# A hybrid encoder trunk on one core: the sample's down products as seven block products per pair of f tiles, and another order of the sample's last norm

## What is computed

```python
D_MODEL = 1024
D_FF = 2816
...
    h = _rmsnorm(x, norm_ffn_g)
    u = jnp.einsum('bsd,df->bsf', h, w_up)
    up = jnp.pad(u, ((0, 0), (1, 1), (0, 0)))
    u = up[:, :-2] * conv_w[0] + up[:, 1:-1] * conv_w[1] + up[:, 2:] * conv_w[2] + conv_b
    a, b = jnp.split(u, 2, axis=-1)
    x = x + jnp.einsum('bsf,fd->bsd', jax.nn.silu(a) * b, w_down)
    return x
...
    return _rmsnorm(x, final_norm_g)
```

## Time and profile before

| | us |
|---|---|
| three runs, median (lowest to highest) | 2393.9 (2391.09 to 2394.6) |
| the profiled execution, its own time | 2391.54 |
| span of the profiled execution | 2389.6 |
| mean granted TensorE clock in it | 0.997 of full speed |

### The profile page before, as it was taken

The page is one execution under the profiler, slowest core; times in us unless marked ns, Lnnn a source line. Parts: engine busy times, 40 slices in busy tenths (PEclk is TensorE's granted clock), DMA queues, the critical chain, the costliest instruction groups (busy, mean ns, idle before and its releaser), DMA issues.

```text
span 2389.6 us, 34203 instructions
## 1 busy us (share of the span) xinstructions
PE 2329.2 (97%) x12186; PEld 1993.3 (83%) x12186; DVE 1798.9 (75%) x2627; ACT 1092.8 (46%) x2147; POOL 1288.7 (54%) x1497
## 2 busy tenths in 40 slices
PE   7999999999999989999999999999989999999998
PEld 6998898888998968888878888888868888888886
DVE  7537777788889967566653379987768888888888
ACT  4426665656678852122332233433244444444444
POOL 5444635588877712043151055555556666666663
PEclk9999999999999999999999999999999999999999
DMA  8744434432222049888873342232253333332332
GB/s 296 250 172 149 159 131 159 154 143 104 79 79 85 13 151 313 305 285 296 281 259 132 106 150 97 89 106 97 84 202 94 97 93 102 93 102 93 100 95 110
DMA packets 153415, 352.69 MB, mean 148 GB/s; under 512 B 15776, under 2 KB 50976, under 8 KB 142752
## 3 DMA queue, kind: packets, MB, share of 16 engines
q1 hardware_dynamic: 151952, 350.12, 43.0%
q10 hardware_dynamic: 1296, 0.39, 0.1%
HBM read 268.67 MB, written 81.79 MB: 147 GB/s over the span
## 4 chain that ended last, share of the span: by engine, by line
PE 57%; DVE 3%; DMA 1%; POOL 1%; issue 1%; SPq 1%; ACT 0%; DVEq 0%; POOLq 0%; ACTq 0%
PE r_bank L2183 29%; PE r_bank L2060 10%; PE r_bank L2089 9%; PE r_bank L2122 5%; PE r_bank L2141 1%; PE r_bank L2170 1%; PE r_bank L2104 1%; DMA r_wxq_raw<-in_w_xq_heads 0%; DVE r_conv L2617 0%; DVE r_block L2610 0%; DVE r_prob L2598 0%; PE r_bank L2153 0%; DVE r_x_p L2833 0%; DVE r_x_p L2850 0%; POOL r_wxq_lo L1900 0%
## 5 line engine op out<-in xcount | busy, mean ns | idle before, releaser
L843 PE MATMUL t_proj<-t_w_hi,t_hbuf 128*128 128x384 f32 x1056 | 311.7, 348 | 2.1 <-ACT t_nat L994 0.7
L2705 DVE TENSOR_TENSOR r_x_p<-r_bank,r_x_p 128x512 f32<-128x512 f32 x280 | 183.0, 683 | 47.9 <-PE r_bank L2183 46.8
L1153 DVE TENSOR_REDUCE t_max_neg<-t_scores 128x1 f32<-128x1024 f32 (+1 forms) x192 | 197.0, 1038 | 23.8 <-PE t_scores L877 17.9
L1017 ACT ACTIVATE t_prob<-t_scores,t_max_neg 128x1024 f32<-128x1024 f32 (+1 forms) x192 | 187.4, 978 | 49.7 <-DVE t_max_neg L1153 45.5
L843 PEld LDWEIGHTS t_proj<-t_w_hi,t_hbuf 128*128 128x128 f32 x1056 | 194.9, 189 | 8.3 <-issue 6.8
L1026 ACT CAST t_pt_hi<-t_turn 128x512 fp32r<-128x512 f32 x240 | 140.3, 587 | 107.5 <-PE t_turn L896 82.3
L1173 DVE TENSOR_TENSOR t_pt_lo<-t_turn,t_pt_hi 128x512 fp32r<-128x512 f32 x240 | 163.5, 686 | 29.9 <-ACT t_pt_hi L1026 26.1
L843 PE MATMUL t_proj<-t_w_lo,t_hbuf 128*128 128x384 f32 x528 | 177.9, 337 | 0.0
L2617 DVE SCALAR_TENSOR_TENSOR r_conv<-r_rows,r_taps,r_conv 128x511 f32<-128x511 f32 (+3 forms) x134 | 157.0, 1172 | 27.0 <-ACT r_conv L2415 24.6
L1933 POOL TENSOR_TENSOR r_w_lo<-r_stage,r_w_hi 128x1024 fp32r<-128x1024 f32 x42 | 100.9, 2403 | 129.3 <-ACT r_w_hi L2354 129.3
L1949 POOL TENSOR_TENSOR r_s_lo<-r_s_raw,r_s_hi 128x512 fp32r<-128x512 f32 x87 | 131.7, 1519 | 63.2 <-ACT r_s_hi L2359 63.2
(11 more groups left out here) (318 smaller groups left out, 7315.2 us busy)
## 6 DMA issues: line engine op xcount, KB each, us to landing
t_hbuf<-split_x SPq DMA_DIRECT2D x60, 1024.0 KB, 4.8
block_sums<-r_block SPq DMA_DIRECT2D x128, 256.0 KB, 3.7
r_block<-in_w_up_units SPq DMA_DIRECT2D x88, 256.0 KB, 5.1
r_stage<-in_w_up_units SPq DMA_DIRECT2D x44, 512.0 KB, 3.3
r_s_raw<-block_sums SPq DMA_DIRECT2D x87, 256.0 KB, 2.7
r_w_raw<-in_w_up_units SPq DMA_DIRECT2D x66, 256.0 KB, 2.6
split_x<-t_hbuf SPq DMA_DIRECT2D x12, 1024.0 KB, 5.3
r_stage<-in_w_down SPq DMA_DIRECT2D x22, 512.0 KB, 3.3
```

Of the source, the lines that this page charges most:

```text
L843: ins = nc.tensor.matmul(proj_bank(i), l, r[:, k, :], start=(k == 0 and j == 0), stop=(k == KT - 1 and j == 2))
L1017: nc.scalar.activation(prob[:, n % PSLOTS, 0:p.keys], ps_s[:, n % 2, 0:p.keys], ACT.Exp, bias=max_neg[:, n % COLS:n % COLS + 1], accum_out ...
L1153: nc.vector.tensor_reduce(max_neg[:, n % COLS:n % COLS + 1], ps_s[:, n % 2, 0:p.keys], AX.X, ALU.max, negate=True).then_inc(max_done, 1)
L2705: nc.vector.tensor_tensor(x_p[:, t, cols], down_bank(q), x_p[:, t, cols], ALU.add).then_inc(p_add, 1)
```

## The change

- Sample's down products of f tiles 0 to 19 are made per pair of f tiles, as seven block products (`sample_pair`): f tiles 2m and 2m+1 by token halves (two tiles of 128 tokens) by column halves, 6 matmuls of 512 columns each. p7, p1, p4 and p6 are woven into the second up product of f tile 2m+2 after blocks 1, 3, 5 and 7, and p5, p2 and p3 into that of f tile 2m+3 after blocks 1, 3 and 5. For the last pair these three stand in the first up product of f tile 21. f tiles 20 and 21 keep the eight plain products.
- Their weights are the block sums that prompt uses too, and plain blocks, 512 wide, through three slots (`sd_raw/hi/lo`): load (`load_s`), cast on ScalarE (`s_high`), low part on GpSimd (`s_low`). A load waits until the product three weights before it is through. `split_down` is gone.
- Their left sides are halves of the gated products, now kept for two f tiles in `s_g`, and four sums of them by GpSimd (`b_sums`, 256 wide), with seven casts (`b_high`, ScalarE) and seven low parts (`b_low`, VectorE), 256 wide, per pair. `sg_hi` and `sg_lo` stay for f tiles 20 and 21 alone.
- VectorE's adds: 14 per pair in place of 16. In f tile 1, which has no down products now, the four operand steps follow each other.
- Last norm: tiles 2 and 3 are squared, scaled and sent first, then 0 and 1, whose scalings stand behind `subtract_w22(1)` and behind the value shifts of f tile 1. Prompt's first down load no longer waits for sent tiles; the next two wait for tile 0 and tile 1. The low part of prompt's first sum (`a_low(0, "s3")`) moves to behind the last scaling.

VectorE in the period of an f tile with operand steps, before: `r_x_s` are the rows added to, L2642 the operand steps, L2665 the gated product, L2668 its low part.

```diff
+S_ORDER = ("p7", "p1", "p4", "p6", "p5", "p2", "p3")
+S_LEFT = [LEFT[p] for p in S_ORDER]
...
+S_SLOTS = (172, 176, 188)
+S_PER = 2 * ND
+S_REST = S_PER * PAIRS
+S_ALL = S_REST + 2 * S_DOWNS
+S_WEIGHTS = ND * PAIRS + 4
+S_WEAVE = ({1: "p7", 3: "p1", 5: "p4", 7: "p6"}, {1: "p5", 3: "p2", 5: "p3"})
...
+            def load_s(m, p):
+                n = s_weight(m, p)
+                if n >= 3:
+                    sp.wait_ge(s_down, 2 * (n - 2) if n <= ND * PAIRS + 2 else S_REST + ST)
+                if m >= PAIRS:
+                    src = a["w_down"][0][m * P:(m + 1) * P, p * BANK:(p + 1) * BANK]
+                elif DOWN_WEIGHT[p] in DOWN_BLOCKS:
+                    src = sums[FT + m][DOWN_BLOCKS.index(DOWN_WEIGHT[p])]
+                else:
+                    f, c = 2 * m + int(DOWN_WEIGHT[p][1]) - 1, int(DOWN_WEIGHT[p][2]) - 1
+                    src = a["w_down"][0][f * P:(f + 1) * P, c * BANK:(c + 1) * BANK]
+                sp.dma_start(sd_raw[n % 3][:, :], src).then_inc(wd_in[n % 3], 16)
...
             def send_sample(t):
-                sp.wait_ge(s_out, t + 1)
-                sp.dma_start(y_rows(SAMPLE[t]), x_s[t][:, :]).then_inc(y_sent, 16)
+                sp.wait_ge(s_out, LEAVES.index(t) + 1)
+                sp.dma_start(y_rows(SAMPLE[t]), x_s[t][:, :]).then_inc(*((y_sent, 16) if t < 2 else (s_room, 16)))
 
...
+            def s_low(m, p):
+                n = s_weight(m, p)
+                pool.wait_ge(wd_rounded, n + 1)
+                nc.gpsimd.tensor_tensor(sd_lo[n % 3][:, :], sd_raw[n % 3][:, :], f32(sd_hi[n % 3][:, :]), ALU.subtract).then_inc(wd_ready, 1)
+
+            def b_sums(m, name):
+                if name == "s3" or name == "s1":
+                    pool.wait_ge(s_prod, 2 * m + (1 if name == "s3" else 2))
+                else:
+                    pool.wait_ge(a_sum, s_sum_of(m, name) - 1)
+                if m:
+                    pool.wait_ge(s_down, s_used(m - 1, name))
+                a11, a21, a12, a22 = b_raw["a11"], s_g[0][:, HB:BANK], b_raw["a12"], b_raw["a22"]
+                x, y, op = {"s3": (a11, a21, ALU.subtract), "s1": (a21, a22, ALU.add), "s2": (b_raw["s1"], a11, ALU.subtract),
+                            "s4": (a12, b_raw["s2"], ALU.subtract)}[name]
+                nc.gpsimd.tensor_tensor(b_raw[name], x, y, op).then_inc(a_sum, 1)
...
+            def sample_pair(m, p):
+                n, w, left = s_weight(m, p), s_weight(m, p) % 3, LEFT[p]
+                before = n - {"p5": 1, "p2": 3}.get(p, 2)
+                pe.wait_ge(wd_ready, n + 1)
+                pe.wait_ge(a_ready, n + 1)
+                if n == 0:
+                    pe.wait_ge(h_hi_done, both)
+                for q in range(2):
+                    if before >= 0:
+                        pe.wait_ge(s_add, 2 * before + q + 1)
+                    tile, place = slice(q * P, (q + 1) * P), one_bank((4 if p in ("p7", "p4", "p2") else 6) + q)
+                    three(place, b_hi[left][:, tile], b_lo[left][:, tile], sd_hi[w][:, :], sd_lo[w][:, :], p in OPENS, True,
+                          p not in OPENS).then_inc(s_down, 1)
 
             for i in range(1, FT):
+                weave = S_WEAVE[i % 2] if i > 1 else {}
                 for k in range(KT):
                     sample_up(i, 0, k)
+                    if i == LAST and k in weave:
+                        sample_pair(PAIRS - 1, weave[k])
                 for k in range(KT):
                     sample_up(i, 1, k)
-                    for n in SAMPLE_WEAVE.get(k, ()):
-                        sample_down(i - 1, n)
+                    if i == LAST:
+                        for n in SAMPLE_WEAVE.get(k, ()):
+                            sample_down(FT - 2, n)
+                    elif k in weave:
+                        sample_pair(i // 2 - 1, weave[k])
...
+            def pair_adds(m, p):
+                n, (part, c) = s_weight(m, p), LANDS[p]
+                if p == "p6":
+                    dve.wait_ge(s_add, 2 * n)
+                for q in range(2):
+                    t, cols = 2 * part + q, slice(c * BANK, (c + 1) * BANK)
+                    dve.wait_ge(s_down, 2 * n + q + 1)
+                    nc.vector.tensor_tensor(x_s[t][:, cols], one_bank((4 if p in ("p7", "p4", "p2") else 6) + q), x_s[t][:, cols],
+                                            ALU.add).then_inc(s_add, 1)
+
+            def b_low(m, name):
+                dve.wait_ge(a_rounded, s_at_step(m, name))
+                if name in ("s1", "s2"):
+                    dve.wait_ge(a_sum, s_sum_of(m, "s2" if name == "s1" else "s4"))
+                nc.vector.tensor_tensor(b_lo[name][:, :], b_raw[name], f32(b_hi[name][:, :]), ALU.subtract).then_inc(a_ready, 1)
 
             def sum_step(k, n):
                 cols = slice(k * BANK, (k + 1) * BANK)
...
+                        low_step(i - SUMS - 1, n)
+
+                if not even and i > 1:
+                    b_low(m, "a12")
+                    b_low(m, "s4")
+                if i == LAST:
+                    for p in ("p5", "p2", "p3"):
+                        pair_adds(m, p)
                 sample_shifts(i, 0)
-
-                def sample_adds(lo, hi):
-                    for n in range(lo, hi if i else lo):
-                        if i == 1 and n == 0:
-                            dve.wait_ge(rows_loaded, 16 * ST)
-                            dve.wait_ge(h_hi_done, both)
+                if i == 1:
+                    dve.wait_ge(h_hi_done, both)
+                    for n in range(4):
+                        operand_step(n)
+                elif i == 2:
+                    dve.wait_ge(rows_loaded, 16 * ST)
+                if even and i:
+                    b_low(m, "a22")
+                    pair_adds(m, "p7")
+                    operand_step(0)
+                    pair_adds(m, "p1")
+                    operand_step(1)
+                    b_low(m, "s2")
+                    b_low(m, "s1")
+                    pair_adds(m, "p4")
+                    operand_step(2)
+                    pair_adds(m, "p6")
+                    operand_step(3)
+                elif i == LAST:
+                    for n in range(6):
                         sample_add(i - 1, n)
-                        if n % 2 and 1 <= i <= SUMS:
-                            sum_step(i - 1, n // 2)
-                        elif n % 2 and SUMS < i <= SUMS + len(H_OPERANDS):
-                            low_step(i - SUMS - 1, n // 2)
-
-                sample_adds(0, 6)
+                elif i:
+                    for n, p in enumerate(("p5", "p2", "p3") if i > 1 else ()):
+                        pair_adds(m, p)
+                        operand_step(n)
+                        if n == 1:
+                            b_low(m + 1, "s3")
+                            b_low(m + 1, "a11")
+                    if i > 1:
...
             add_s2(0)
-            sample_mean(0)
-            sample_mean(1)
+            sample_mean(2)
+            sample_mean(3)
             add_s3_s1(0)
             edge_shifts(0)
             subtract_w22(0)
-            dve.wait_ge(s_gain, 16)
+            dve.wait_ge(s_room, 16)
             dve.wait_ge(row_rstd, 1)
-            sample_scale(0)
+            sample_scale(2)
             add_s4(0)
             value_shifts(0)
             gated(0, edge, edge_silu, edge_prod)
-            sample_mean(2)
-            sample_mean(3)
-            sample_scale(1)
+            sample_mean(0)
+            sample_mean(1)
+            sample_scale(3)
...
                 subtract_w22(i)
-                if i == LAST:
+                if i == 1:
+                    dve.wait_ge(row_rstd, 2)
+                    sample_scale(0)
+                    value_shifts(i)
+                    sample_scale(1)
+                    a_low(0, "s3")
```

305 lines of the change are left out of this document (199 added, 106 removed).

## The result

| | before | changed |
|---|---|---|
| median of 18 runs each, us | 2393.2 | 2396.8 |
| lowest to highest, us | 2391.1 to 2395.9 | 2393.8 to 2405.9 |
| span of the profiled execution, us | 2389.6 | 2394.5 |
| mean granted clock in it | 0.997 | 0.993 |

The ratio is 1.0022, interval 1.0014 to 1.0029: slower by 3.6 us, less than the 4.8 us that the prediction took as the least that can be told, and inside the range. Where the time goes is another matter: two terms of the sum were wrong, by 12.5 and by 7 us, in opposite directions. One run of a kernel further down (e11_best), at a granted clock of 0.835 from end to end and 2612.5 us long, is left out of its numbers.

What follows compares the result with a forecast made beforehand. TensorE, busy 97% of the span, was taken as the bound, VectorE next with 0.77 us left in periods with operand steps. -13.6 + 16.1 + 9.3 - 4.9 = +6.9 us gave 2400 us, range 2385 to 2411.

Steps and rivals of the forecast that it cites:

- the prediction's own sign: It called itself wrong if a pair takes 31.3 us throughout, instead of 34.1 us from f tile 2 on.
- first rival: In the pairs VectorE keeps up: 0 to 3 us instead of 16.1, 2385 to 2388 us; chance 0.28.
- second rival: The clock falls at the new waits of 4.7 and about 4.5 us: +5.2 us, 2406 us; chance 0.17.
- Matmuls, -13.6 us: Sample's down products: 42 matmuls a pair instead of 48, 60 fewer in ten pairs at 0.2267 us each.
- VectorE in the pairs, +16.1 us: Standing SBUF instructions make TensorE wait 2.9 us at even f tiles 4 to 12, 1.8 at tile 2; bounds 0 and 24.
- The free sum of 23.4 us: VectorE's work in a pair with operand steps without standing: 14 additions, 8 shifts and 17 SBUF instructions.
- The bound that I had from the operand steps' own row, 0.41: Lower bound for standing per SBUF instruction of VectorE: 30.4 us a pair, so TensorE never waits.
- f tile 2, +1.8 us of it: TensorE waits 1.8 us at f tile 2's second up product, since four operand steps stand in one piece.
- The four waits, +9.3 us: Last two f tiles and handover: waits of 2.5, 2.3, 1.1 and 4.7 us, less 1.3; bounds 6 and 12.
- The clock: Granted clock falls to 0.50 behind waits from about 5 us on: +5.2 us if both do; chance 0.17.
- The norm, -4.9 us: Last norm: the 5.57 us wait goes and s3's chain for tile 2 starts earlier, 1785.6 for 1790.54; bounds 0 and -8.
- The loads' cover of 1.9 us: In the pairs, weights waiting for slots are costed at nothing, with cover 1.9 us; later landings lose what lies above.

Runs made afterwards that it cites:

- e11_best: e10_spread with the order of e4_tail at f tiles 20 and 21 and add_s4(1) ahead of the value's conv shifts of f tile 1: 2378.9 us, 0.9934.
- e9_doubled: e6_spaced with each of VectorE's seven half-width subtractions per pair made once more into a spare tile: 2417.8 us in one run.
- e10_spread: Changed kernel with no operand steps in f tile 1 and the 28 low parts spread over f tiles 6 to 19, two each: 2391.2 us, 0.9989.
- e8_lighter: Changed kernel with GpSimd's low parts of the up weights of f tiles 3 to 19 over 16 of 1024 columns, result wrong: 2396.1 us in one run.
- e4_tail: Changed kernel with casts, weight loads and low parts reordered at f tiles 20 and 21 alone: 2387.7 us, 0.9973.
- e1_norm: Kernel before with the new order of the last norm alone, sample's down products left plain: 2391.2 us, 0.9991.
- e2_pairs: Changed kernel with the old order of the last norm, so the seven block products alone: 2404.8 us, 1.0042.
- e3_tile1: Changed kernel with two of the four operand steps of f tile 1 moved behind the gated product: 2395.8 us, 1.0013.
- e6_spaced: Changed kernel with the last two operand steps of each odd f tile from 1 to 11 behind the gated product: 2400.3 us, 1.0032.
- e7_joint: e6_spaced with the order of e4_tail, add_s4(1) ahead of the value shifts, and prompt's row loads behind those of s4 and s3: 2391.8 us, 0.9997.

## Why the prediction was right, and where not

The number was right, and the way to it in good part not. By the prediction's own sign (wrong if a pair takes 31.3 us throughout) its first rival came true for the pairs: VectorE keeps up there from f tile 3 on. What would have made the kernel faster than forecast was used up by slow clock, the second rival, and mostly behind waits that I hadn't named for it. That the total lands near 2400 us is luck. Term by term:

- **Matmuls, -13.6 us:** as forecast. 12186 matmuls became 12126, and 138 of them take 31.28 us.
- **VectorE in the pairs, +16.1 us:** the term that failed. It came to 3.6 us before f tile 2 and nothing in f tiles 4 to 12 in the profiled execution. The free sum of 23.4 us was right (a half-width subtraction takes 0.41 us when free, 0.34 from start to start); the standing wasn't: (29.7 - 23.4) / 17 = 0.37 us each and not 0.63. The bound that I had from the operand steps' own row, 0.41, was the nearer value. In the trace GpSimd stands too: 23.6 us a pair where I had 21.2, its 512-wide low parts 1489 ns where 1290 are free. e9_doubled shows that TensorE does wait for VectorE once VectorE's work is over the period; the changed kernel's pairs are 0.09 us per instruction short of that (0.37 for 0.46).
- **The price per instruction** was itself the wrong measure. By the same free costs, VectorE stands 6.3 us a pair over 17 instructions with operand steps, 25.2 - 18.5 = 6.7 over 9 without them, 28.7 - 21.0 = 7.7 over 13 in e10_spread, and before, from the earlier trace rows, 31.1 - 23.6 = 7.5 over 12 and 24.5 - 18.7 = 5.8 over 4. These are estimates, but they show no growth with the number of VectorE's instructions. With less work on GpSimd (e8_lighter, 13 to 15 us a pair for 23) it is 4.8 and 4.7 us. Taken as 6 to 7.5 us a pair, the standing would have given 29.4 to 30.9 us, and no wait in the pairs.
- **f tile 2, +1.8 us of it:** the four operand steps in one piece made 3.45 us, and e10_spread, which has none there, has no wait in f tile 2.
- **The four waits, +9.3 us:** 9.8 us without the clock, and e4_tail takes all but 2.1 us away by order alone.
- **The clock:** the term that I had as a rival with 0.17, from waits of about 5 us on, for 5.2 us. It cost 7.1 us, behind waits of 3.45, 2.24 and 4.16 us, so the 5 us were wrong.
- **The norm, -4.9 us:** measured -2.9 by the account and -2.0 by e1_norm. The place was right, and of the mechanism only a half: the waits themselves hardly shrank, 7.9 to 7.5 us, since three of 0.6, 5.6 and 1.2 us were replaced by five of 0.8 to 2.7. What went is the slow clock behind it, 3.0 to 0.5 us, which the sum hadn't counted as a gain.
- **The loads' cover of 1.9 us:** held; the changed kernel's pairs have no wait of TensorE at all from f tile 3 on. But where VectorE and GpSimd meet seems to hang on landings (the rows of f tile 7 above), which the prediction didn't see at all.

So the total, 2400 for 2396.8 us, is right through errors that cancel: 12.5 us too much for VectorE; too little by 7.1 us of clock, 2.0 of the norm, 0.5 of the four waits and 1.0 in the rest of the program. That leaves 1.9, from +6.9 to +5.0. The medians differ by 3.6 and the two profiled executions by 5.1, since the one of before was 1.7 us faster than its kernel's median.

## What to carry to other kernels

Two engines that keep each other out are not priced by a mean per instruction: here one stood 6 to 8 us in a period whether it had 4 or 17 such instructions in it, and less when the other engine had less work. Where such an engine has under 2 us of room in 31, give the tight stretch less work (here two steps fewer in each of f tiles 6 to 11); shifting work about inside it only moved the wait to GpSimd. When a change shortens a periodic schedule, look at the ends of the loop: here 15.6 us were lost at the last two tiles, and all but 2.1 of them went by an order in which each engine serves the next thing wanted. And price a wait with the clock behind it: 22.1 us of waits brought 7.7 us of slow clock here.

## What the runs showed of the hardware

- In the changed kernel the granted clock fell to 0.50, its lower level, behind waits of 3.45 and 4.16 us and, 1 us later, behind one of 2.24 us, and stayed at 1.00 behind one of 2.23 us, 12 us later, and one of 2.73 us. Such a fall cost 0.2 us on each of 8 to 13 matmuls.
- The length of the wait alone doesn't decide it. The wait of 2.24 or 2.25 us before p2 was followed by 0.50 in the changed kernel and in e10_spread, and by 1.00 in e2_pairs, e3_tile1, e6_spaced and e8_lighter, where TensorE has the same matmuls there. The shortest wait with a fall behind it was 1.80 us (e10_spread, at 1797.87), the longest without one 2.97 us (e9_doubled, at 1409.03). What decides, these runs don't tell.
- Where a DMA had landed 0.28 us sooner, two VectorE instructions took 4.42 us instead of 1.28.
- The landing of one 512 KB sending took 10 us behind eight row loads of that size (e7_joint); the same sending took 4.2 us in the changed kernel.
